# Four projections fed a quarter of the features at a time, w_ada in column quarters with six slots

## The reference

```
mod = silu(c) @ w_ada + b_ada                       # c: 1 x 1024, w_ada: 1024 x 6144
shift_m, scale_m, gate_m, shift_f, scale_f, gate_f = split(mod, 6)
h = rmsnorm(x, g_mix_pre) * (1 + scale_m) + shift_m # 256 x 1024
z = h @ w_in                                        # q, k, v, forget logits, pool, conv, 3 gates
log_f = log_sigmoid(fl + b_f); cum_f = cumsum(log_f)
logits = q k^T * scale + cum_f[q] - cum_f[k]        # 8 heads, causal, softmax, times v
... pool mixer and short convolution, gated sum, w_out, feed forward, second layer
```

## Time and profile before

| what | value |
|---|---|
| median of three timed runs | 882.52 us |
| profiled execution | 884.4 us |
| span of its trace | 883.2 us |
| TensorE busy | 808.3 us, 92% |
| VectorE busy | 565.6 us, 64% |
| ScalarE busy | 416.8 us, 47% |
| mean granted TensorE clock | 0.964 |

### The profile page before, as it was taken

How to read it: one execution, slowest core, us unless ns; L and a number is a source line. 1 busy time by engine, 2 the same in 40 slices (tenths; PEclk the granted TensorE clock), 3 DMA queues, 4 the chain that set the end, 5 groups by cost and what they waited for, 6 DMA issues and landing times.

```text
span 883.2 us, 13000 instructions
## 1 busy us (share of the span) xinstructions
PE 808.3 (92%) x5292; PEld 736.4 (83%) x5292; DVE 565.6 (64%) x786; ACT 416.8 (47%) x610; POOL 74.9 (8%) x127
## 2 busy tenths in 40 slices
PE   2599899999992999999999999899988899999995
PEld 2589789899972999999988999778977799999994
DVE  5677697657965446656657698948434665555563
ACT  3344256545344354444447457647443644444441
POOL 4400670000301000000001000010000100000000
PEclk9999899899995999999999999999989999999998
DMA  9877577658572346555655654445523355555541
GB/s 311 293 268 240 202 251 258 221 193 287 186 237 72 122 165 214 167 196 186 191 191 168 191 161 148 144 143 168 190 78 113 120 190 191 189 186 187 186 160 47
DMA packets 83051, 163.70 MB, mean 185 GB/s; under 512 B 5152, under 2 KB 5344, under 8 KB 82992
## 3 DMA queue, kind: packets, MB, share of 16 engines
q1 hardware_dynamic: 80800, 156.26, 53.9%
q10 hardware_dynamic: 1696, 5.86, 1.9%
q0 software_dynamic: 496, 0.76, 0.4%
HBM read 161.81 MB, written 1.05 MB: 184 GB/s over the span
## 4 chain that ended last, share of the span: by engine, by line
PE 76%; ACT 8%; DVE 7%; DMA 5%; issue 3%; POOL 1%; SPq 0%; ACTq 0%; DVEq 0%; POOLq 0%
PE bank L1601 23%; PE bank L1602 22%; PE bank L1603 22%; DMA raw_ring<-in_w_in 3%; ACT hi_ring L461 3%; DVE lo_ring L868 2%; DVE ada_acc L897 2%; PE bank L1744 1%; DMA gates<-in_w_ada 1%; PE bank L1638 1%; DMA ada_ring<-in_w_ada 1%; PE bank L1749 1%; PE bank L2051 1%; DVE x_residual L971 1%; PE bank L2072 1%
## 5 line engine op out<-in xcount | busy, mean ns | idle before, releaser
L868 DVE TENSOR_TENSOR lo_ring<-raw_ring,hi_ring 128x1024 fp32r<-128x1024 f32 x248 | 305.6, 1236 | 221.2 <-ACT hi_ring L461 220.8
L461 ACT CAST hi_ring<-raw_ring 128x1024 fp32r<-128x1024 f32 x248 | 259.5, 1049 | 361.6 <-PE bank L1603 339.1
L1601 PE MATMUL bank<-h_hi,hi_ring 128*128 128x256 f32 x1008 | 292.1, 290 | 18.6 <-DVE post_rows L954 9.4
L1602 PE MATMUL bank<-h_lo,hi_ring 128*128 128x256 f32 x1008 | 289.2, 287 | 0.0
L1603 PE MATMUL bank<-h_hi,lo_ring 128*128 128x256 f32 x1008 | 288.9, 287 | 0.0
L1601 PEld LDWEIGHTS bank<-h_hi,hi_ring 128*128 128x128 f32 x1008 | 197.6, 196 | 20.9 <-issue 10.0
L1602 PEld LDWEIGHTS bank<-h_lo,hi_ring 128*128 128x128 f32 x1008 | 197.7, 196 | 0.9 <-issue 0.2
L1603 PEld LDWEIGHTS bank<-h_hi,lo_ring 128*128 128x128 f32 x1008 | 197.4, 196 | 0.0
L1601 PE MATMUL bank<-hi_ring,branch_hi 128*128 128x512 f32 x320 | 125.7, 393 | 2.8 <-DVE branch_lo L1009 2.7
L1602 PE MATMUL bank<-lo_ring,branch_hi 128*128 128x512 f32 x320 | 124.7, 390 | 0.0
L1603 PE MATMUL bank<-hi_ring,branch_lo 128*128 128x512 f32 x320 | 124.6, 389 | 0.0
(11 more groups left out here) (257 smaller groups left out, 920.2 us busy)
## 6 DMA issues: line engine op xcount, KB each, us to landing
raw_ring<-in_w_ff SPq DMA_DIRECT2D x128, 512.0 KB, 3.6
raw_ring<-in_w_in SPq DMA_DIRECT2D x64, 512.0 KB, 4.3
ada_ring<-in_w_ada SPq DMA_DIRECT2D x40, 512.0 KB, 4.9
raw_ring<-in_w_out SPq DMA_DIRECT2D x16, 512.0 KB, 3.6
raw_ring<-in_w_xkv SPq DMA_DIRECT2D x16, 512.0 KB, 3.7
gates<-in_w_ada SPq DMA_DIRECT2D x8, 512.0 KB, 7.6
raw_ring<-in_w_branch SPq DMA_DIRECT2D x8, 512.0 KB, 4.8
raw_ring<-in_w_xq SPq DMA_DIRECT2D x8, 512.0 KB, 3.5
```

What stands on the lines that cost most here:

```text
L461: act.copy(m.hi[:, m.slot(u)], m.raw[:, m.slot(u)]).then_inc(s.hi_done, 1)
L868: dve.tensor_tensor(m.lo[:, m.slot(u)], m.raw[:, m.slot(u)], as_f32(m.hi[:, m.slot(u)]), ALU.subtract).then_inc(s.lo_done, 1)
L1601: pe.matmul(out, a_hi, b_hi, start=start, stop=False, skip_group_check=True)
L1602: pe.matmul(out, a_hi, b_lo, start=False, stop=False, skip_group_check=True)
```

## The change

The first 16 units are taken a quarter of the features at a time: for each 256 features one unit of v, q, k and pool, in that order. `w_ada`'s first 16 loads come in quarters too, as 256 columns of shift_m and 256 of scale_m, each by its own DMA of 256 KB. `x` moves from one DMA of ScalarE to the head of SyncE's list, as two DMAs. Six slots hold `w_ada` instead of four and then two. Four of them lie in `mem_k` and `mem_v`. The 32 later loads are worked off over units 16 to 51. v is written out once a quarter and added on VectorE three times. The forget logits stand after unit 14, the `cum_f` products ahead of the first scores, in bank 6, the head pairs one step later, and the pool products after unit 31. Two row sums (`ada_row`, bias and gain rows for gate_m and gate_f) move on VectorE: gate_m's from unit 21 to unit 25, gate_f's from behind the first unit of the feed-forward into the output projection.

```diff
-ATT1_AT = (0, 7, 13, 20)
+ATT1_AT = (1, 8, 14, 21)
-ADA_FIRST, ADA_UNITS = 16, 48
-ADA_ORDER = (0, 2, 1, 3, *range(4, 12))
+ADA_FIRST, ADA_UNITS, ADA_RING = 16, 48, 6
+FIRST_SLABS = (2, 0, 1, 3)
...
+    if a < ADA_FIRST:
+        return [rows[:, c0 + c * S:c0 + c * S + S].rearrange("(k p) n -> p k n", p=P) for c0 in (0, D)]
...
+    for tt in range(NT):
+        sp.dma_start(m.x[:, tt, :], t["x"][0][tt * P:tt * P + P, :]).then_inc(s.x_in[tt], DMA)
+    for a in range(RING):
         load_ada(a)
     load(0)
+    for q in range(1, RING):
+        a, u = RING * q, RING * (q - 1)
         load_ada(a)
+        load_ada(a + 1)
+        load(u + 1)
+        load_ada(a + 2)
+        load(u + 2)
+        load_ada(a + 3)
+        load(u + 3)
+        load(u + 4)
...
+    affine_quarter(0)                                   # ScalarE
+    for q in range(RING - 1):
+        u = RING * q
+        hi(u + 1)
+        hi(u + 2)
+        if q == 0:
+            act.wait_ge(s.used, 1)
+            for tt in range(NT):
+                act.copy(m.v_tok[:, tt, :], bank[4 + tt][:, :]).then_inc(s.v_part, 1)
+        hi(u + 3)
+        affine_quarter(q + 1)
+        hi(u + 4)
...
-            if i == 13:
+            if i == 11:                                 # pool products, on ScalarE, VectorE, TensorE
...
+    for _ in range(KD):                                 # VectorE
         ada()
     norm_columns(0, 0)
+    lo(0)
+    for q in range(RING - 1):
+        u = RING * q
+        for _ in range(2 * UK):
+            ada()
+        lo(u + 1)
+        for _ in range(UK):
+            ada()
+        lo(u + 2)
+        if q:
+            add_values(q)
+        for _ in range(UK):
+            ada()
+        lo(u + 3)
+        norm_columns(q + 1, 4)
+        lo(u + 4)
...
+            if n == 1 and j == 2:
+                ada_row(s.ff_row_ps, s.ff_rows_in, s.ff_row, m.rows[:, 1, :], 2)
...
     affine_lo(s.ff1t)
     after(FF1 - 1)
-    ada_row(s.ff_row_ps, s.ff_rows_in, s.ff_row, m.rows[:, 1, :], 2)
...
+    norm_columns(0, 0)                                  # TensorE
+    for q in range(RING):
+        for j, i in enumerate(FIRST_SLABS):
+            u = RING * q + j
+            if j == RING - 1 and q < RING - 1:
+                norm_columns(q + 1, 4)
+            if j == 0:
+                pe.wait_ge(*s.xm.lo.at(q + 1))
+            if i == 2:
+                claim(4, 5)
+                tokens(u, UK * q, m.h_hi, m.h_lo, 4, True, True)
+            else:
+                features(u, q, m.h_hi, m.h_lo, 2 * i)
+            if u == 14:
+                forget_logits()
```

More of the change, by code:

```diff
@@ L83, in ada_slot @@
 def ada_slot(a):
-    return (a % 4, a // 4 + 1) if a < ADA_FIRST else (a % 2, 4 + (a - ADA_FIRST) // 2 + 1)
+    return a % ADA_RING, sum(2 if b < ADA_FIRST else 1 for b in range(a % ADA_RING, a + 1, ADA_RING))
 def unit_sources(t):
@@ L107, in unit_sources @@
     columns = (0, UN, 2 * UN, 3 * NH * DH + NH)
-    units += [unit(w_in, j * UK * P, columns[i]) for _, i, j in first_units()]
+    units += [unit(w_in, j * UK * P, columns[i]) for j in range(RING) for i in FIRST_SLABS]
     for s in range(1, 8):
@@ L215, in __init__ @@
         self.hi_done, self.lo_done, self.used = new("hi_done"), new("lo_done"), new("used")
-        self.ada_in = [new(f"ada_in{j}") for j in range(4)]
+        self.ada_in = [new(f"ada_in{j}") for j in range(ADA_RING)]
         self.ada_used = new("ada_used")
@@ L1054, in dve_program @@
     after(9)
     after(10)
-    take_half(12, 3, pair(m.kT, 2), s.k_out)
+    add_values(3)
     after(11)
+    after(12)
+    take_half(14, 1, pair(m.qT, 2), s.q_out)
+    after(13)
+    take_half(15, 3, pair(m.kT, 2), s.k_out)
     dve.wait_ge(s.fl_ps, 1)
@@ L1067, in dve_program @@
     own.then(dve.tensor_scalar(m.tmp16[:, 2, :], flz, 0.0, None, ALU.min))
-    after(12)
-    dve.wait_ge(s.used, 14)
-    for tt in range(NT):
-        v = m.v_tok[:, tt, :]
-        dve.tensor_tensor(v, v, bank[4 + tt][:, :], ALU.add).then_inc(s.v_out, 1)
+    after(14)
+    take_half(16, 7, pair(mix, 2), s.mixA_out)
     dve.wait_ge(s.fl_ln, 1)
@@ L1730, in pe_program @@
[L1730 to L1738 removed]
+        pe.wait_ge(s.ada_used, RING * q + RING)
@@ new lines, in norm_columns, with forget_logits @@
+        ada_columns(q, 1, b).then_inc(s.mix_cols_ps, 1)
+        free[b] = s.mix_cols, 2 * q + 1
+    def forget_logits():
+        pe.wait_ge(s.q_out, 2)
+        pe.wait_ge(s.small_in, SMALL_LOADS * DMA)
+        for tt in range(NT):
+            for k in range(KD):
+                mm = pe.matmul(bank[0][:, tt * NH:tt * NH + NH], m.h_f32[:, k, tt * P:tt * P + P], m.w_fl[:, k, :],
+                               start=(k == 0), stop=(k == KD - 1))
+        mm.then_inc(s.fl_ps, 1)
+        free[0] = s.fl_out, 1
@@ new lines, in cumulative @@
+    def cumulative():
+        claim(6)
+        pe.wait_ge(s.nlogf, 1)
+        pe.wait_ge(s.upper_r_ok, 1)
+        upper = as_f32(m.upper[:, 0:P])
+        b = bank[6]
+        pe.matmul(b[:, 0:NH], upper, m.nlogf8[:, 0, :], start=True, stop=True)
+        pe.matmul(b[:, NH:2 * NH], m.ones[:, :], m.nlogf8[:, 0, :], start=True, stop=False)
+        pe.matmul(b[:, NH:2 * NH], upper, m.nlogf8[:, 1, :], start=False, stop=True).then_inc(s.cum_ps, 1)
+        free[6] = s.cum_out, 1
+    norm_columns(0, 0)
@@ L1784, in attention1 @@
                 if g == 0:
+                    cumulative()
                     pe.wait_ge(s.q_out, 2)
```

226 lines of the change are left out of this document (85 added, 141 removed).

## The result

The changed kernel takes 862.2 us (median of 4 runs, 860.3 to 862.6) where the kernel before, run beside it, takes 882.9: a ratio of 0.976, 95% interval 0.974 to 0.978. It is faster by 20.7 us. The forecast was 866. The profiled execution took 862.5 us with a span of 861.2. One of the four runs of a later experiment, `w_ada` dealt around the copies, took 1009.8 us at a granted clock of 0.743 and is left out of its figures.

A forecast was written before the change was run, and what follows sets the result against it. TensorE is busy nearly throughout, so only the opening and a few stalls up to 237 us can move. Terms -7.3 - 6.3 - 3.3 = -16.9 take the profiled 884.4 to 867.5, or 866 as median; 8 in 10: 858 to 877.

The forecast's parts named there:

- The opening: Start of unit 0: with less loaded ahead of the first columns, the first matmul moves from 32.55 to 19.9, by 12.6 us.
- The quarters: First 16 units: 5.3 of the 12.6 us are given back at the borders; unit 15 ends at 83.7, 7.3 us less.
- The first rival: Quarter borders: the clock falls at each, +5, 871 (0.20, shared with later gain lost); if lasting, 891 (within slower's 0.08).
- The `cum_f` products: First scores: TensorE's 3.4 us wait for VectorE's copy and 2.9 lost to the clock go; -6.3 us, bounds 0 and -6.3.
- in the same slack: Two moved row sums on VectorE: four operations each, some 3 us, covered by its slack; uncovered, 3.
- the -3.3 up to unit 51: Pool products after unit 33: a 1.1 us prob_T wait, 0.9 in products, 1.6 at the lower clock; bounds 0 and -3.6.
- the bound of 7 for the uncovered case: Units 16 to 51: VectorE's denser w_ada, 0.2 us a unit more, costs 7 us if TensorE's units don't cover it.

The follow-up runs named there:

- `w_ada` dealt around the copies: Changed kernel with two w_ada operations in each of units 16 to 51, but none in the four whose low part precedes a prob_T copy: 859.3 us, ratio 0.970.
- the border experiment: Changed kernel, ScalarE rounding the next quarter's first unit before applying the columns, VectorE making its low part meanwhile: 856.3 us, ratio 0.971.
- the old place: Changed kernel with the cum_f products and first pair's scores one unit earlier, after unit 16 instead of 17, still in bank 6: 861.7 us, ratio 0.978.

## Why the prediction was right in its sum and wrong in two of its steps

**The opening** was right in size: columns at 16.2, first matmul at 20.31 against 19.9. Its reason was only half right. I let the last load's end and the last pair set the columns. In the trace VectorE waits for the first load of `w_ada` until 8.0, and then its eight operations run without a gap to 14.2, so behind the first load it is VectorE that sets them, and the other loads are ahead. The short rows cost nothing that shows in time. The Trainium skill ("DMA: Bandwidth & Descriptors", Rules for kernel authors) wants 1 MiB or more in a DMA; the halves of 256 KB, with rows half as long, run at 348 GB/s here, 6% less than pieces of 512 KB.

**The quarters** were right step by step: 15.9, 15.2 and 16.0 us for the 16.4, 15.2 and 15.7 predicted, a wait of 1.55 us at each border for the 1.6, and the chain that I worked out is what the border experiment shortened. Unit 15 missed by 1.8 us. 0.4 of that is the first matmul. The rest is that the forget logits took 4.2 us for the 3.5 and that the whole of unit 15 ran at the lower clock (its matmuls start 0.21 us apart), where I had put it between the two levels.

**The first rival** did not happen: the clock stayed at 1.00 over all three borders. The Trainium skill ("TensorE: Matmul & The Clock Gate", HAM oscillation — how this bites in real kernels) tells of waits for loads in every step, of some 3 to 5 us, that bring the lower clock back in every step; waits of 1.55 us each quarter did not. The border experiment did have a fall inside the third quarter, at 53.1, behind a wait of 1.7 us, so such waits are not shown to be harmless in general.

**The `cum_f` products** gained 6.4 us in their stage, as said. What did it was both that the scores no longer claim the products' bank and that they come a unit later: bank 4 again costs 4.9 us at unit 18, the old place 2.7. But the term does not last in full: at unit 51 the bank is worth 2.1, and the kernel with the old place is 1.0 ahead.

**The step that failed outright** is the sentence that the two moved row sums lie "in the same slack", priced at nothing, or 3 us uncovered. I asked what they cost VectorE and not who waits for what they read. gate_f's sum frees banks 2 and 3, and its move is worth 9 to 10 us at unit 60, shown from both sides.

**The second failed step** is the -3.3 up to unit 51, with the cover for VectorE's denser `w_ada`. The pool products did shrink from 2.07 to 1.0 us, but with them and the three pairs back at their old places the stretch from unit 18 to unit 51 took no longer (1.0 us less). "TensorE's units cover it" was wrong: busy 100 of 129 us is an average, and right before a copy of `prob_T` VectorE had no slack. TensorE waited 4 us for such copies, and dealing the same operations otherwise gave 3.5 us back. With the bound of 7 for the uncovered case in place of nothing, the term would have been 3.7 us lost, nearer to the 1.4 that were.

So 3.3 us didn't come, 1.4 were lost and unit 15 was 1.8 late: 6.5 us the wrong way. The row sum gave 8.9 that were not expected, and the clock late in the kernel 2.9. With some tenths elsewhere this makes the 5 us between the profiled 862.5 and the 867.5 that the prediction's sum gave. That the forecast lies so near is in part luck: errors of 6.5 and 11.8 us went opposite ways, and no term of mine foresaw the late 2.9.

## What to carry to other kernels

When an instruction is moved, price it by what it frees as well as by what it costs: look up who claims its buffer next, and read the list of waits to the end for a line that names it. A stage's busy share does not say whether an in-order engine is covered; look at what stands ahead of the one instruction that another engine waits for, and deal optional work around it. A gain in front of such a place can be eaten by it: compare the same unit's end at several places down the trace before a term is believed.

## What the runs showed that I had not expected

- The first four microseconds of unit 0 ran at half speed while the window from 20.3 to 25.1 reads 1.00: its matmuls of 512 columns start 0.43 us apart until 24.29, and 0.23 apart after. The trace's record of the clock begins only there, with a rise to 1.00 at 24.3, and the window counts what has no record as 1.00. In the kernel with the scores' place changed the record begins at 13.0, and the same window reads 0.69. The record of the kernel before begins at 37.8, where its matmuls go from 0.21 us apart to 0.12, so the 0.94 in the earlier trace rows is too high. The windows, of the changed kernel and of the one with the scores' place:

```profile
20.30:25.10 4.80, 4.79 (x13) 3.79 (x14) 4.59 (x7) 2.07 (x2) 4.07 (x12) 1.00 1.09 350
20.30:25.10 4.80, 4.68 (x17) 3.89 (x18) 4.59 (x7) 1.16 (x2) 4.08 (x12) 0.69 1.09 353
```

- The same `w_ada` pair on VectorE took 1.5 us at 36 us in the kernel before and 2.25 at 107 to 113 in the changed one, when GpSimd was busy for 10.15 of 12 us. Whether GpSimd is the cause was not tried.
- From the first feed-forward unit on, the time has two values 2.7 us apart (580.4 and 583.0), by the clock between 615 and 695 us, in kernels whose code is the same there.
